# One tile of an expert layer routed inside the mixing stage before it

## The reference

```
h    = rms_norm(x);  p = h @ w_in                       # retention and stick-breaking inputs, gates
x   += (gates0 * (ret_o @ w_ret_o) + gates1 * (sb_o @ w_sb_o)) @ w_out
hb   = rms_norm(x)                                      # "h2" below
q    = (hb @ w_pq).reshape(n, 8 heads, 2 sides, 128)
s    = einsum('nhpc,phkc->nhpk', q, pk_keys)            # 16 x 128 scores of a token
v1, i1 = top_k(s[:, :, 0], 16);  v2, i2 = top_k(s[:, :, 1], 16)
sc, sel = top_k(v1[..., :, None] + v2[..., None, :], 16)   # of the 256 sums of a head
e    = (i1 * 128 + i2)[sel];  g = softmax(sc)           # 128 experts of 16384 for each token
a    = gelu(einsum('nhkd,nd->nhk', peer_u[e], hb))      # 128 gathered rows, 128 dots
x   += einsum('nhk,nhkd->nd', g * a, peer_v[e]);  y = rms_norm(x)
```

## Time and profile before

| | |
|---|---|
| median of 3 runs | 4309.09 us (4308.17 to 4321.79) |
| the profiled execution's own time | 4310.76 us |
| its span in the trace | 4309.2 us |
| PE busy | 3726.5 us, 86% |
| DVE busy | 2608.9 us, 61% |
| ACT busy | 816.9 us, 19% |
| POOL busy | 1519.2 us, 35% |

### The profile page before, as it was taken

One profiled execution on the slowest core, in us unless ns is written; L12 is line 12 of the kernel. 1 busy time (PEld: TensorE's weight loads), 2 busy tenths in 40 slices (PEclk: granted clock), 3 DMA queues, 4 the chain that ended last, 5 costly groups with the idle time before them and its releaser, 6 DMA issues.

```text
span 4309.2 us, 40490 instructions
## 1 busy us (share of the span) xinstructions
PE 3726.5 (86%) x14136; PEld 2688.4 (62%) x14136; DVE 2608.9 (61%) x5503; ACT 816.9 (19%) x1469; POOL 1519.2 (35%) x1247
## 2 busy tenths in 40 slices
PE   7999997898996997133899986999968999879999
PEld 6887785455553997122666765667756667556666
DVE  4111102443341588998986989878979879886400
ACT  3111102334332111232000422003410014120000
POOL 0000000000000067675564663565645646645300
PEclk9999997999998999555999998999989999989999
DMA  4222215323232399877899996999978999969844
GB/s 174 86 85 85 82 47 200 121 101 127 88 105 83 122 314 336 288 253 273 304 392 366 367 398 216 395 409 349 374 285 339 394 360 370 385 233 409 312 150 140
DMA packets 321868, 1068.09 MB, mean 248 GB/s; under 512 B 51664, under 2 KB 54800, under 8 KB 319600
## 3 DMA queue, kind: packets, MB, share of 16 engines
q0 software_dynamic: 179520, 654.00, 41.1%
q1 hardware_dynamic: 137712, 391.66, 25.0%
q10 hardware_dynamic: 4480, 20.45, 1.2%
HBM read 1003.20 MB, written 62.78 MB: 247 GB/s over the span
## 4 chain that ended last, share of the span: by engine, by line
PE 30%; DVE 16%; DMA 14%; POOL 3%; issue 3%; ACT 1%; SPq 0%; ACTq 0%; DVEq 0%
PE pair L1791 24%; DMA e_vr<-in_peer_v 8%; DVE e_ur L1563 7%; DMA e_ur<-in_peer_u,e_eidx 6%; POOL e_ur L1293 3%; PE pair L1761 2%; PE pair L1721 2%; DVE e_hot L1648 2%; DVE e_hot L1643 1%; DVE e_sc L1470 1%; DVE e_found L1527 0%; DVE e_sc L1522 0%; DVE e_sc L1525 0%; ACT e_hot L1387 0%; DVE e_oh L1632 0%
## 5 line engine op out<-in xcount | busy, mean ns | idle before, releaser
L1791 PE MATMUL pair<-e_vr,e_region 128*128 128x512 f32 x4096 | 1830.2, 603 | 34.0 <-DMA e_vr<-in_peer_v 33.2
L1293 POOL DMA_INDIRECT e_ur<-in_peer_u,e_eidx x1088 | 1388.3, 1276 | 1147.9 <-DVE e_dots L1563 819.1
L1791 PEld LDWEIGHTS pair<-e_vr,e_region 128*128 128x128 f32 x4096 | 1190.6, 296 | 611.0 <-DMA e_vr<-in_peer_v 132.1
L1563 DVE CUSTOM_DVE_ANT_0 e_ur<-e_ur,e_h 128x1024 f32<-128x1024 f32 x1088 | 1303.7, 1224 | 254.0 <-DMA e_ur<-in_peer_u,e_eidx 245.2
L1761 PE MATMUL pair<-e_hot 128*128 128x128 f32 x2048 | 340.3, 323 | 244.5 <-issue 105.7
L1761 PEld LDWEIGHTS pair<-e_hot 128*128 128x128 f32 x2048 | 312.3, 230 | 310.8 <-issue 177.8
L400 PE MATMUL pair<-w_hi,h_hi 128*128 128x512 f32 (+1 forms) x936 | 366.0, 391 | 0.7 <-issue 0.6
L400 PE MATMUL pair<-w_lo,h_hi 128*128 128x512 f32 (+1 forms) x936 | 365.1, 390 | 0.0
L400 PE MATMUL pair<-w_hi,h_lo 128*128 128x512 f32 (+1 forms) x936 | 364.8, 390 | 0.0
L269 DVE COPY out_sb<-pair 128x512 f32<-128x512 f32 x52 | 35.9, 691 | 419.0 <-PE pair L400 411.9
L1398 ACT ACTIVATE e_region<-pair 128x512 f32<-128x512 f32 x256 | 152.6, 597 | 689.5 <-PE pair L1761 689.3
(11 more groups left out here) (216 smaller groups left out, 3043.0 us busy)
## 6 DMA issues: line engine op xcount, KB each, us to landing
e_vr<-in_peer_v SPq DMA_DIRECT2D x512, 512.0 KB, 6.7
w<-in_w_in POOLq DMA_DIRECT2D x13, 2048.0 KB, 9.4
proj<-out_sb SPq DMA_DIRECT2D x104, 256.0 KB, 2.0
e_ur<-in_peer_u,e_eidx POOLq DMA_INDIRECT x1088, 7.9
V<-proj POOLq DMA_DIRECT2D x36, 256.0 KB, 3.0
gates<-proj SPq DMA_DIRECT2D x8, 1024.0 KB, 4.8
e_region<-in_w_pq SPq DMA_DIRECT2D x4, 2048.0 KB, 15.3
sc_d<-e_region ACTq DMA_DIRECT2D x16, 512.0 KB, 6.0
```

Of the source, the lines that this page charges most:

```text
L1293: pool.indirect_dma_start(ur[:, m % U_RING, :], None, peer_u[0], bass.IndirectOffsetOnAxis(ap=eidx[:, n % 3, k:k + 1], axis=0))\
L1563: dve.tensor_tensor_reduce(ur[:, m % U_RING, :], ur[:, m % U_RING, :], h2[:, n % 2, :], 1.0, 0.0, ALU.mult, ALU.add, dots[:, n % 2, k:k + ...
L1791: last = pe.matmul(acc[t][:, c], blocks[:, at, :, i % 64], vr[:, no % V_RING, c], start=False, stop=True, skip_group_check=True)
```

## The change

The first prompt tile (tile 0 of `experts`, merged in mix tile n = 2) gets its queries, scores and routing inside `mix`; the 25 routing parts move to a function that both stages call. The buffers that both need (`vr`, `sc`, `top`, `best`, `eidx`, `gate` and others) are made in a class `Head` that outlives `mix`.

- In `mix` both hardware loops become Python loops, so every tile and block has its own instructions. `az` now is the buffer `kT`, `wT` is `pT`, `ra` gives way to `rb` and `rot`, and the square's unused output goes to PSUM.
- End of mix tile 1: PE turns the keys (16 transposes from `vr`), ACT copies them and stores them to `keysT_d`.
- End of mix tile 2 (`Q_TILE`): PE multiplies 16 slabs of w_pq (512 KB each, ring of three) with `turnedT`, ACT copies, PE makes the key scores, ACT copies them to `sc`.
- Mix tiles 3 to 7: five routing parts each on DVE, between `skT` and `pT`; ACT's `exp_gates(0)` at the end of tile 5.
- `experts` starts with h2 and the transposed h2 of tile 1, then w_pq in quarters, the turned keys behind the second; PE computes queries of tiles 1 to 8 only. POOL's gathers and DVE's dots of tile 0 wait for no routing.
- Routing of tile 1 stands at dots 66 to 121 of tile 0; `hots` of the first filling at every second dot of tile 1 from dot 62. Routing part 14 of tile 2 also waits for `turn_keys(0, 0)`.

```diff
@@ mix @@
-            with eng.Fori(2, TILES) as n:
+            for n in range(2, TILES + 1):
                 tile(n, P, n - 1, P)
-            tile(TILES, P, TILES - 1, P)
...
+                def query_slab(i):
+                    if i >= V_RING:
+                        sy.wait_ge(s["w_used"], i - V_RING + 1)
+                    elif i == 0:
+                        sy.wait_ge(s["keysT_out"], 32)
+                    half, k = divmod(i, KD)
+                    sy.dma_start(E.vr[:, i % V_RING, :],
+                                 keysT_d[k] if half == 2 else w_pq[0, k * P:(k + 1) * P, half * D:(half + 1) * D])\
+                        .then_inc(w_in[i % V_RING], 16)
...
+                def turned_keys():
+                    act.wait_ge(s["keys_turned"], 2)
+                    for half, ps, at in ((0, pair[0], 2), (1, pair[1], 0)):
+                        act.activation(E.vr[:, at, :], ps[:, :], ACT.Copy).then_inc(s["keysT_rdy"], 1)
+                        act.wait_ge(s["keysT_rdy"], half + 1)
+                        act.dma_start(keysT_d[half], E.vr[:, at, :]).then_inc(s["keysT_out"], 16)
+
+                def turned_queries():
+                    for half in range(2):
+                        act.wait_ge(s["w_used"], KD * (half + 1))
+                        act.activation(pqT[half][:, :], pq_ps[half][:, :], ACT.Copy).then_inc(s["pqT_rdy"], 1)
+                    for half in range(2):
+                        act.wait_ge(s["ps_rdy"], half + 1)
+                        act.activation(E.sc[:, half * HALF:(half + 1) * HALF, :], in_blocks(pq_ps[half][:, :]), ACT.Copy)\
+                            .then_inc(E.scores_rdy, 1)
...
                     dve.tensor_copy(h4(skT[:, :], rows), h4(skT_ps, rows)).then_inc(s["skT_rdy"], 1)
+                    if n > Q_TILE:
+                        for p in range((n - Q_TILE - 1) * A_PARTS, min(PARTS, (n - Q_TILE) * A_PARTS)):
+                            routing(dve, E, C, route, 0, p)
                     dve.wait_ge(s["scores_rdy"], n + 1)
...
@@ PE, a tile of mix @@
+                    if n == Q_TILE + 1:
+                        pe.wait_ge(E.scores_rdy, 1)
+                    if n == 2:
+                        pe.wait_ge(s["keysT_rdy"], 1)
                     turn(pair[0], rot, rows, 8).then_inc(s["qk_turned"], 1)
...
+                def queries(n):
+                    pe.wait_ge(s["ret_rdy"], HEADS * (n + 1))
+                    for half in range(2):
+                        for k in range(KD):
+                            i = half * KD + k
+                            pe.wait_ge(w_in[i % V_RING], w_loaded(i))
+                            for j in range(HALF):
+                                last = pe.matmul(pq_ps[half][:, j * P:(j + 1) * P],
+                                                 E.vr[:, i % V_RING, j * P:(j + 1) * P], turnedT[:, k, :], ...)
+                            last.then_inc(s["w_used"], 1)
+                    for half in range(2):
+                        i = 2 * KD + half
+                        pe.wait_ge(s["pqT_rdy"], half + 1)
+                        pe.wait_ge(w_in[i % V_RING], w_loaded(i))
+                        for j in range(HALF):
+                            last = pe.matmul(pq_ps[half][:, j * P:(j + 1) * P], pqT[half][:, j * P:(j + 1) * P],
+                                             E.vr[:, i % V_RING, j * P:(j + 1) * P], ...)
+                        last.then_inc(s["ps_rdy"], 1)
@@ experts @@
-    HALVES = 2 * NT
+    HALVES = 2 * TILES
...
-                load_hT(0)
+                for n in range(2):
+                    sy.dma_start(h2[:, n, :], h2_d[x2_rows(n), :]).then_inc(h2_in[n], 16)
+                load_hT(1)
                 for i, c in enumerate(quarters):
                     sy.dma_start(wpq[:, :, c], w_pq[0].rearrange("(k p) n -> p k n", p=P)[:, :, c])\
                         .then_inc(w_in[i], 16)
...
+                def first_parts(k):
+                    return min(PARTS, max(0, k - 66) * PARTS // 56)
+
+                def first_hots(k):
+                    return min(BATCHES, max(0, k - 60) // 2)
...
-                for p in range(PARTS):
-                    routing(0, p)
...
                         if n == 0:
-                            if k >= 6 and k % 4 == 2 and (k - 6) // 4 < PARTS:
-                                routing(1, (k - 6) // 4)
+                            for p in range(first_parts(k), first_parts(k + 1)):
+                                routing(dve, E, C, route, 1, p)
                         elif n % 2 == 1:
...
+                                if g == 0 and (k - 4) // 4 == 14:
+                                    dve.wait_ge(s["keys_rdy"], 1)
+                                routing(dve, E, C, route, n + 1, (k - 4) // 4)
+                            if g == 0:
+                                for m in range(first_hots(k), first_hots(k + 1)):
+                                    hots(0, 0, m)
+                            elif k >= H_FROM and (k - H_FROM) % 3 == 0 and (k - H_FROM) // 3 < BATCHES:
                                 hots(g, 0, (k - H_FROM) // 3)
```

More of the change, by code:

```diff
@@ L130, in __call__, with __init__ @@
             eng.sem_inc(self.passed, 1)
+LAST = TILES
+S_DOTS = SLOTS * SAMPLE // P
+HALF = SIDES // 2
+PARTS = 25
+class Head:
+    def __init__(self, sb, sem):
+        self.vr = sb("vr", [P, V_RING, D])
+        self.vr_in, self.slabs = [sem(f"h_vr_in{i}") for i in range(V_RING)], 2 * KD + 2
+        self.sc = sb("sc", [P, SIDES, KEYS])
+        self.top = sb("top", [P, SIDES, TOPK])
+        self.topi = sb("topi", [P, SIDES, TOPK], U32)
+        self.best = sb("best", [P, PHEADS, TOPK])
+        self.besti = sb("besti", [P, PHEADS, TOPK], U32)
+        self.part = sb("part", [P, 3, SLOTS])
+        self.found = sb("found", [P, 2, PHEADS, TOPK])
+        self.sums = sb("sums", [P, PHEADS])
+        self.eidx = sb("eidx", [P, 3, SLOTS], U32)
+        self.gate = sb("gate", [P, 2, SLOTS])
+        self.own, self.owned = sem("h_own"), 0
+        self.scores_rdy, self.scores_in = sem("h_scores_rdy"), sem("h_scores_in")
+        self.best_rdy, self.exp_rdy, self.gates_rdy = sem("h_best_rdy"), sem("h_exp_rdy"), sem("h_gates_rdy")
@@ L529, in past_blocks @@
             elif later(n):
-                with eng.Fori(1, n) as j:
+                for j in range(1, n):
                     block(block_no(n) + j, j)
@@ L594, in tile @@
                             past_blocks(sy, n, lambda b, j: keys(b, n, j))
+                        if n == Q_TILE:
+                            for i in range(V_RING):
+                                query_slab(i)
                         store_rows(m, m_rows)
@@ L597, in tile @@
                     sy.dma_start(x[r, :], x_sample[0] if first(n) else x_prompt[0, at, :]).then_inc(s["x_in"], 16)
+                    if n == Q_TILE:
+                        for i in range(V_RING, 2 * KD + 2):
+                            query_slab(i)
                 def store_rows(n, rows):
@@ L1180, in experts @@
         u_in = [sem(f"c_u_in{i}") for i in range(U_RING)]
-        v_in = [sem(f"c_v_in{i}") for i in range(V_RING)]
+        v_in = E.vr_in
         def tokens(n):
@@ L1213, in arrived, with v_arrived @@
             return 16 * (no // ring + 1)
+        def v_arrived(no):
+            return arrived(no, V_RING) + 16 * E.slabs // V_RING
         def x3(n):
@@ L1251, in _ @@
                         .then_inc(w_in[i], 16)
-                load_hT(1)
-                for n in range(2):
-                    sy.dma_start(h2[:, n, :], h2_d[x2_rows(n), :]).then_inc(h2_in[n], 16)
+                    if i == 1:
+                        for half in range(2):
+                            sy.dma_start(pkT[:, half * HALF:(half + 1) * HALF, :],
+                                         keysT_d[half].rearrange("p (s k) -> p s k", k=KEYS)).then_inc(s["keys_in"], 16)
                 for n in range(2, NT):
@@ L1317, in _ @@
                 act.preload_act_table_set(ACT_TABLE)
-                for half in range(2):
-                    act.wait_ge(s["keys_turned"], half + 1)
-                    act.activation(pkT[:, half * 8:half * 8 + 8, :], in_blocks(pair[half + 1][:, :]), ACT.Copy)\
-                        .then_inc(s["keysT_rdy"], 1)
                 def q_copy(m):
@@ L1428, in _ @@
                         s_copy(m - 1)
-                    if m == 5:
-                        exp_gates(0)
-                    elif m == 6:
+                    if m == 2:
                         load_scores(1)
@@ L1551, in chosen @@
-                def chosen(n):
-                    if n < LAST:
-                        return [(slice(0, P), SLOTS, lambda ap: ap)]
-                    return [(slice(i * SAMPLE, (i + 1) * SAMPLE), S_DOTS,
-                             lambda ap, i=i: ap.rearrange("p (h two) k -> p two h k", two=2)[:, i]) for i in range(2)]
+                route = gelu = norm = prep = small = Chain(dve, E.own, E.owned)
                 def dot(n, k):
```

357 lines of the change are left out of this document (185 added, 172 removed).

## The result

The kernel became slower. The median is 4336.17 us (six runs, 4329.30 to 4340.09), and of the kernel before on the same chip 4315.20 us (six runs, 4308.17 to 4326.05): a ratio of 1.0045, with a 95% interval of 1.0027 to 1.0063. The forecast was 4293, its range 4264 to 4324. The profiled execution took 4331.8 us, its span is 4330.1 against 4309.2.

What follows compares the result with a forecast made beforehand. PE was taken to bound the mix and DVE the expert stage's start. Mix costs 37 + 7 + 5 - 3 = 46 and gains of 62 gave -16 us on 4310.76, so 4294.8, median 4293; range 4264 to 4324.

Steps and rivals of the forecast that it cites:

- S': Start of the expert stage in the changed kernel's trace, 1445.46 us; times after it are written S'+.
- S: Start of the expert stage in the kernel before, 1392.48 us; forecast times in that stage are written S+.
- Tile 1 itself: Expert stage, tile 1: shifted `hots` fill DVE's idle time, about 8, less waits of 3 and 1; gain 4 us.
- Sharing the DMA engines half and half with the gathers, it takes twice that: Expert stage start: w_pq's 27 us double beside the gathers, last quarter about S+55, first queried tile's end 17.5 us later.
- the stage's gain: Expert stage up to tile 1's first dot: from S+363.7 to S+306, a gain of 58 us.
- the second rival: Expert stage start: w_pq starved at a third of the engines, last quarter S+86, gain 31 against 46, 4324; chance 0.14.
- The queries: Mix tile 2: records 28.9, key scores 3.6, slab waits 4, copies 0.5; cost 37 us, ends 33 and 51.
- The late `pT`: Mix tiles 3 to 7: routing parts make `pT` late by 0.9 and 3.7 us, otherwise hidden; cost 5 us.
- the unrolled loops: Mix: loops made plain code take 3 us off for six tiles; ends 10 off and 3 on.
- the keys: Mix, end of tile 1: turning the keys makes PE's next turns wait for ACT; cost 7 us, ends 4 and 14.
- the two halves: Both sides of the forecast: the mix pays 46 us, the expert stage gains 62 us.
- the ring's 15: Mix tile 2: waits added by the three-slab ring if slabs land after 7.0 us, instead of the 4 taken.

Runs made afterwards that it cites:

- Rows of 4 KB: The changed kernel with w_pq loaded in rows of 4 KB instead of 2 KB, PE taking tile 1's products contraction outermost: 4326.48 us, ratio 1.0015.
- w_pq ahead of the gathers: The changed kernel with GpSimd's first gather waiting for w_pq's last quarter: 4295.87 us, ratio 0.9950 to the kernel before.
- ScalarE's order: The changed kernel with tile 1's gate exp, tile 2's score load and tile 0's GELU exp moved inside ScalarE's query loop: 4277.01 us, ratio 0.9905.

## Why the prediction was wrong

*What bounds the kernel, and what is moved:* right. The first dot is at S'+7.9 (S+6 forecast). Routing hides in the mix but for two late `pT`, of 0.7 and 3.5 us (0.9 and 3.7 forecast). Tile 1 itself gave 3.1 (4 forecast). It was also right that DVE would wait at part 23 for ACT's exponential.

*The step that failed* is "Sharing the DMA engines half and half with the gathers, it takes twice that". Half of the packets is what SP's queue with w_pq got, but its rows are half as long, so of the bytes it got 36%. The last quarter was there at S'+80, not S+55; the first queried tile ended at S'+89.2, not S+63 (its last 64 records took 9.4 us where 8 were counted). With 4.7 us more behind the second tile's hT, the exponential came at S'+325.8, not S+294.5, so 31 of the 34 us that the stage's gain fell short come from this step; the rest passed between the exponential and the dot, 13.8 us for 11.4. With w_pq's rows as long as the gathers' 20.4 us of it were gone, with hT's some 10. With about half of the bytes PE's last 128 records began at S'+52, near the forecast, so it was the share that was wrong and not what was made of it. DVE was at part 23 earlier than forecast, at S'+252 instead of S+266, which lengthened its wait and not its end. The sum also left out the turned keys, 1 MB behind w_pq's second quarter on the same queue: at 1.42 MB in 10 us an estimated 7 us. PE's wait for the third quarter, 10.22 us beside 4.45 and 4.80, points to them; no run moved them. What happened in this stage is the second rival nearly to the number: a third of the engines, last quarter at S+86, gain 31 (measured 36%, S'+80, 27). It had a chance of 0.14. Rows of 4 KB and w_pq ahead of the gathers show the cause; ScalarE's order shows that the exponential's place behind the last copy cost this stage 63.5 us, of which the forecast had 28.

The rule of the Trainium skill named in the prediction (DMA: Bandwidth & Descriptors, Queues, rings and completion order: each DMA engine takes a packet from each queue row in turn) is the one that the traces bear out in the count, 710 packets against 711; how many rows make one turn the count does not show. I had the packet's length before me, w_pq's 2 KB, and took the half share because hT had landed in 4.5 us among gathers. That row is of loads of 256 KB; here 8 MB stood in one queue, and a row of small loads says nothing of the share that a long one gets.

*The mix, mis-sized:* 53.0 against 46. The queries cost 43.0 instead of 37: the waits for slabs were 5.4 us where I took 4, and PE's slower records behind them cost 3.4, half of it at the lower clock, for which I had nothing. Another 1.6 were a wait for the second half of the turned keys. The late `pT` cost 8 with the clock instead of 5, the unrolled loops gave nothing instead of 3, the keys 6.4 of 7. Of the term's size not all is the kernel's: in five executions with this same mix the stage began at 1439.1 to 1447.6, so 47 to 55 later than before.

*The sum* had -62 + 46. Measured: -24.1 - 3.1 + 53.0 = +25.8 at tile 2's first dot, of which 5 are gone by the end; where they went stays open. The forecast also stood on the kernel before at 4309.09, the median of three runs; the six beside the result have 4315.20. So of the 43 us between 4293 and 4336.17, 42 are the two halves and 6 the base, less those 5. Some ends do not come out of their terms: the queries with the ring's 15 are 48, not 51; the parts of the mix give 32 to 73, not 30 to 71; the better ends of both halves, 79 and 30, give 4260, not 4264. The 4293 rests on none of them.

## What to carry to other kernels

A load put beside a stream of gathers got packets here, not bytes: compare the row lengths of the two queues before taking a share. When a producer becomes late, look at what stands behind it in order on the engine that passes its result on: here moving three short steps forward from behind the last copy made the kernel some 60 us faster. Before filling an engine's idle time with work from elsewhere, ask whether what it waits for is itself at its limit.

## What the runs showed of the hardware

Packets of two DMA queues went one for one over ten microseconds, whether the rows of one were 2 KB or 4 KB (710 and 711, 537 and 536), and over two with mostly 256 B on one side (177 and 178); not in the four in which the first gathers came in (262 and 1425). DMA engines that are busy do not always move the same bytes: at a share of 1.02 to 1.08 (the sum of packet times) two queues of long rows reached 401 and 409 GB/s, and gathers beside rows of 256 B 338 GB/s, from 1450 to 1454 us of the changed kernel.

Behind a wait of 3 us in the mix, PE's granted clock fell from the higher of its two levels (2.4 GHz) to the lower (1.2) in some executions and not in others. With the same wait of 3.46 us for `pT` in tile 5 it fell in three of six: in the changed kernel it was 0.50 from 1062.0 to 1068.8, in the kernel with ScalarE's order 1.00 over that whole tile. Behind the wait of 2.66 us for a slab it was at the lower level for 3.4 us.
